# Added products of x in TensorE's order at the norms, the routing and the first gathers of a two-layer decoder trunk

## The reference

```python
def block(x, c, pos, p, cache):
    mod = (jax.nn.silu(c) @ p['w_ada'] + p['b_ada'])[:, None, :]
    shift1, scale1, gate1, shift2, scale2, gate2 = jnp.split(mod, 6, axis=-1)
    h = rmsnorm(x, p['g_norm1']) * (1.0 + scale1) + shift1
    mixed, new_state = token_mixing(h, pos, p, cache)
    x = x + gate1 * mixed
    h = rmsnorm(x, p['g_norm2']) * (1.0 + scale2) + shift2
    x = x + gate2 * hier_moe(h, p['w_router_grp'], p['b_router_grp'], p['w_router_exp'], p['b_router_exp'],
                             p['w_exp_gate'], p['w_exp_up'], p['w_exp_down'])
    return x, new_state
```

## Time and profile before

| | us |
|---|---|
| median of three runs | 2113.04 |
| lowest and highest of them | 2104.05 and 2121.15 |
| the profiled execution's own time | 2108.11 |
| its span from the first to the last instruction | 2106.3 |
| TensorE busy in it | 1872.1 (89%) |
| mean granted clock | 0.931 |

### The profile page before, as it was taken

How to read it: one execution, slowest core, us unless ns; L and a number is a source line. 1 busy time by engine, 2 the same in 40 slices (tenths; PEclk the granted TensorE clock), 3 DMA queues, 4 the chain that set the end, 5 groups by cost and what they waited for, 6 DMA issues and landing times.

```text
span 2106.3 us, 24153 instructions
## 1 busy us (share of the span) xinstructions
PE 1872.1 (89%) x9680; PEld 953.8 (45%) x9680; DVE 555.9 (26%) x1246; ACT 368.5 (17%) x673; POOL 35.3 (2%) x59
## 2 busy tenths in 40 slices
PE   4799667898999999999969994778799999999995
PEld 2477534454444444444436772334444444444442
DVE  0164355533001111011035543554300111101103
ACT  1121134312111010110113102433101101111011
POOL 0000100000000000000000001000000000000000
PEclk9899789889699999999989996989879999999998
DMA  9622389939699999999952208984439999999991
GB/s 399 262 101 71 117 323 342 347 143 365 252 417 375 400 376 382 370 384 392 376 204 80 80 18 295 342 324 185 160 143 416 371 402 375 376 379 369 403 380 82
DMA packets 111863, 609.74 MB, mean 289 GB/s; under 512 B 13219, under 2 KB 15524, under 8 KB 49922
## 3 DMA queue, kind: packets, MB, share of 16 engines
q1 hardware_dynamic: 108690, 595.77, 71.7%
q0 software_dynamic: 3056, 12.35, 1.8%
HBM read 602.26 MB, written 5.81 MB: 289 GB/s over the span
## 4 chain that ended last, share of the span: by engine, by line
PE 75%; SPq 10%; DMA 6%; DVE 4%; issue 3%; ACT 1%; POOL 1%; DVEq 0%; POOLq 0%; ACTq 0%; PEldq 0%
PE PS L1013 31%; PE PS L980 11%; PE PS L591 10%; PE PS L992 7%; SPq L467 5%; SPq L457 4%; PE PS L927 3%; DMA ring<-in_w_ada 3%; PE PS L523 2%; PE PS L549 1%; PE PS L535 1%; DMA ring<-in_w_down 1%; SPq L490 1%; DMA ring<-in_pool_kv 1%; DVE big L1480 1%
## 5 line engine op out<-in xcount | busy, mean ns | idle before, releaser
L1013 PE MATMUL PS<-ring,big 128*64 128x512 f32 x3072 | 680.3, 597 | 6.6 <-ACT big L1152 6.0
L1013 PEld LDWEIGHTS PS<-ring,big 128*64 128x64 f32 x3072 | 214.6, 137 | 427.1 <-issue 418.1
L1152 ACT ACTIVATE big<-PS 128x512 f32<-128x512 f32 (+8 forms) x202 | 145.7, 731 | 1122.1 <-PE PS L1013 394.1
L1480 DVE TENSOR_TENSOR big<-big,PS 128x320 f32<-128x320 f32 (+4 forms) x172 | 88.1, 519 | 741.2 <-PE PS L992 429.0
L980 PE MATMUL PS<-big 128*128 128x256 f32 (+1 forms) x768 | 239.3, 443 | 2.9 <-DVE big L1930 2.2
L591 PE MATMUL PS<-mT,ring 128*128 128x320 f32 x768 | 216.3, 441 | 0.0
L980 PEld LDWEIGHTS PS<-big 128*128 128x128 f32 (+1 forms) x768 | 135.4, 203 | 103.1 <-issue 91.2
L591 PEld LDWEIGHTS PS<-mT,ring 128*128 128x128 f32 x768 | 146.8, 193 | 63.3 <-issue 6.2
L992 PE MATMUL PS<-big 128*128 128x320 f32 x512 | 145.8, 438 | 2.2 <-ACT big L1152 2.2
L992 PEld LDWEIGHTS PS<-big 128*128 128x128 f32 x512 | 94.8, 190 | 62.5 <-issue 22.7
L523 PE MATMUL PS<-cst,big 128*128 128x128 f32 (+4 forms) x472 | 80.5, 296 | 10.5 <-DVEq L389 9.4
(11 more groups left out here) (287 smaller groups left out, 1229.5 us busy)
## 6 DMA issues: line engine op xcount, KB each, us to landing
ring<-in_w_gate SPq DMA_DIRECT2D x128, 1024.0 KB, 9.5
ring<-in_w_up SPq DMA_DIRECT2D x128, 1024.0 KB, 8.7
ring<-in_w_down SPq DMA_DIRECT2D x128, 1024.0 KB, 7.7
ring<-in_pool_kv SPq DMA_DIRECT2D x256, 256.0 KB, 8.7
ring<-in_w_ada SPq DMA_DIRECT2D x48, 1024.0 KB, 14.0
big<-in_windows SPq DMA_DIRECT2D x16, 2432.0 KB, 8.5
ring<-in_w_in SPq DMA_DIRECT2D x24, 1024.0 KB, 7.2
ring<-in_w_out SPq DMA_DIRECT2D x8, 1024.0 KB, 8.6
```

The lines of the kernel that those rows point to most:

```text
L1013: i = mm(PS[SLOTS * x:SLOTS * x + SLOTS, out_bank + half, :], stationary(k, x), w, start=(k == 0), stop=(k == steps - 1))
L1152: return nc.scalar.activation(out, in_, ACT.Copy)
L1480: return V.tensor_tensor(out, a, b, op)
```

## The change

A new function `keep_warm(n)` issues n products of 128 by 128 and 512 columns of x, whose result goes to bank 7 and is read by nobody. They stand in TensorE's list in layer 1 before the tail product (7), before the router product (6), behind the second and the third block of turned rows (2 and 4) and before the first gather (2); in layer 0 before the first gather (4). They wait for nothing. No instruction is taken away, and the other engines' lists stay as they are.

```diff
--- before.py
+++ after.py
@@ -529,6 +529,11 @@
                 half_full(slot, count)
                 pe.wait_ge(ring_full[slot], count * 16)
 
+            def keep_warm(n):
+
+                for _ in range(n):
+                    mm(PS[:, 7, :], xT_[:, 0:128], xT_[:, 0:512], start=True, stop=True)
+
             def add_squares(n, k):
 
                 pe.wait_ge(sem["sq"], KT8 * n + k + 1)
@@ -575,6 +580,8 @@
                     for k in range(KT8):
                         add_squares(2 * l, k)
                 pe.wait_ge(loads, l * LOADS + LOADS_A)
+                if l:
+                    keep_warm(7)
                 for k in range(KT8):
                     pe.wait_ge(sem["h_done"], 2 * KT8 * l + k + 1)
                     i = mm(PS[0:36, 4, 0:T], wtail[:, k, :], mT[:, k, :], start=(k == 0), stop=(k == 7))
@@ -932,6 +939,8 @@
                 add_squares(2 * l + 1, 7)
                 if l == 0:
                     pe.wait_ge(sem["proj_ev"], 32)
+                else:
+                    keep_warm(6)
                 next_mods(3)
                 if l == 0:
                     pe.wait_ge(sem["mod_rows_kept"], 14)
@@ -949,6 +958,8 @@
                     for k in range(KT8):
                         i = tr(PS[0:n, (5, 0, 5)[t] + k // 4, (k % 4) * 128:(k % 4) * 128 + 128], mT[:, k, t0:t0 + n])
                     i.then_inc(sem["rows_turned"], 1)
+                    if l and t:
+                        keep_warm(2 * t)
                 next_mods(2)
                 pe.wait_ge(sem["selected"], l + 1)
 
@@ -967,7 +978,10 @@
                 next_mods(5)
                 if l == 0:
                     mod_turn(23)
+                    keep_warm(4)
                     pe.wait_ge(sem["mods_kept"], 1)
+                else:
+                    keep_warm(2)
                 pe.wait_ge(sem["gates_kept"], l + 1)
                 for part in ((0, 1), (2, 3), (4, 5, 6, 7)):
                     gather(GROUPS * l, part)
```

## The result

| | us |
|---|---|
| before, median of 20 runs | 2113.47 (2101.33 to 2129.41) |
| changed, median of 20 runs | 2086.59 (2080.30 to 2105.66) |
| ratio, with its 95% interval | 0.9869 (0.9849 to 0.9889) |
| profiled execution, before and changed | 2108.11 and 2089.32 |

The change makes the kernel 1.3% faster, and the whole interval lies beyond 1%. The forecast was 2080 in 2070 to 2098.

The account below looks back on a forecast made before the run. TensorE's own work and waits were taken to bound the kernel, with both first gathers at half clock. Gains of 1.9 + 3.2 + 11.9 + 1.4 + 9.6 = 28.0 us took 2108.1 to 2080 us, range 2070 to 2098.

Parts of the forecast that it names:

- The gathers: First gather of each layer: added products keep the clock high, 13.4 us each, gaining 11.9 (layer 1) and 11.5 us (layer 0).
- weights are loaded between the records: Both first gathers: the reason given why 25.3 against 13.4 us is less than a factor of two.
- The second norm and the selection: Layer 1 before the gather: router product 4.50 us instead of 6.68, products 0.6 us too long, ranks' end 3.2 us earlier.
- Layer 0: Four products on the path before its first gather: net gain between 8.4 and 10.8 us, taken as 9.6.
- the list of what the profile would show: Signs expected in the profile after; for layer 0, the added products take 3.5 to 5.6 us.
- The gate products: Behind the first gathers: first 64 gate records at 13.95 us, gaining 1.4 us in layer 1 and 2.1 in layer 0.
- Too short for a fall: Behind layer 1's first gather: 1.97 us of idle TensorE during ScalarE's copy would not lower the clock.
- The tail product: First norm of layer 1: seven hidden products make it 4.50 instead of 6.40 us, 1.9 us gained, ends 0 to 2.1.
- Layer 0 paid: Rival, chance 0.10: the clock falls during layer 0's four products, which cost 2.8 to 5.2 us and bring nothing; 2094 us.
- the clock held through 13.5 us of gather: Rival, chance 0.05, said the opposite: the high clock doesn't hold through a gather of full length; 2107 us.
- the transfers didn't hold up the first group: Rival, chance 0.04, said the opposite: late weight blocks make layer 0's first group wait, taking back its gain; 2090 us.
- The added products never all ran at 1.2 GHz: Rival, chance 0.03, said the opposite: added products run at 1.2 GHz, 1.74 us each, making the kernel slower; 2129.5 us.

## Why the prediction was right

**The gathers: right, and the size too.** The step gave 11.9 and 11.5 us. The profile after has 13.56 and 13.46 us, so 11.7 and 11.5. The Trainium skill's halving (TensorE: Matmul & The Clock Gate, Terms), 12.65 and 12.5, is a little too much here. The prediction's reason, that weights are loaded between the records, is not shown: the gather's weight loads were themselves busy 13.38 us at the low level and 7.77 at the high one. The two experiments that put the levels side by side (inside one gather, and 9 against 512 columns) show the cause.

**The second norm and the selection: right.** The router product took 4.50 us as said. From the last squares to the ranks the stretch shrank from 22.44 to 20.47 us (the step had 20.9), and to the gather from 29.40 to 25.70: 3.7 us gained for a step of 3.2. The products started 0.43 us a record apart, as priced. The selection's copy now ended at 1514.21 and the ranks began at 1514.48. The products were thus 0.3 us too long, not 0.6.

**Layer 0: the mechanism right, the term a little large.** The step had the products start at the high clock and take 3.5 us, or 5.9 where it falls under them (5.6 in the list of what the profile would show). In the profile after the clock was already at 0.50, and they took 5.85. The gather waited for them, and with the gate products the place gave 7.0 us of the step's 9.6: 6.7 of 7.5 ahead of the gate products, 0.4 of 2.1 in them. In the kernel with them alone, where they started high and the gate products kept the clock, it gave 10.9, the upper end of the step; its 9.6 lies between.

**The gate products: wrong.** "Too short for a fall" is the step that failed, 1.4 and 2.1 us in the sum. Of the 2.1 in layer 0 the profile after has 0.4, and in layer 1 the gate products got 0.3 us slower. In the profile after, 1.97 us of idle TensorE was followed by a fall in both layers, 15.65 us each; over all profiles with a gather that ended at the high level and no products behind it, the clock was lost at nine places of ten (15.40 to 16.97 us) and kept at one (13.95). With two added products in the gap it was kept at six of six, at one of them through 1.97 us of idle time all the same.

**The tail product: wrong half the time.** "Far below the 4.1 us that left the clock at 1.00" judged by the length of a gap alone. The same 1.96 us lost the clock in two profiles of four and kept it in two. The 1.9 us are worth about half of that on average; nine products in place of seven made it 4.50 in three of three.

**The sum.** Its parts were 28.0 us and the medians differ by 26.9. The profiled executions alone differ by 18.8: the changed places gave 22.35, and the rest is other stretches that happened to be slower. That 28.0 lies so near 26.9 is in part luck: it holds 3.5 us of gate products and 1.9 of tail product, of which the profile after gave 0.1 and 0.2. The predicted time was nevertheless 6.6 us low, mostly because I added nothing for the 4.9 us by which the profiled execution before lay under the median. My reason, that the two large falls make the scatter and go away, was wrong. The gathers were slow in every profile without dense work ahead, so they added no scatter, and the runs after spread over 25 us, as they did before over 28.

**The rivals.** Layer 0 paid, the clock held through 13.5 us of gather, and the transfers didn't hold up the first group: ScalarE's copy released it in both layers. The added products never all ran at 1.2 GHz. Where the only two did (3.78 us), they still paid.

## What to carry to other kernels

A busy TensorE says nothing of its level: look at the granted clock over each stretch, and for streams whose records are slower than the same form elsewhere. A stream can be unable to bring the clock back and yet keep it, so a few dense products ahead of it can be worth far more than they cost: here 3.78 us of added work took 10.9 us off a gather and 10.7 off the median. What sets the gather apart from the dense products, its 256 columns, its weight loads or something else, no run separates. Put such products first where a wait hides them, and size them by the wait. Two more in the short gap behind the gather kept the clock every time in the profiles; the time doesn't show their gain.

## What the runs showed of the hardware

- A gather busy for 25.20 of 25.20 us (the kernel with 9 columns) stayed at 0.50 all the time. Two dense products in front of it, 3.60 us at 0.50, were enough to have it at 0.93 over its length.
- The same idle gap of 1.96 us behind the same seven products kept the clock in two profiles and lost it in two, while 4.1 us at the second norm had left it at 1.00. And 1.97 to 2.12 us behind a gather lost it at nine places of ten, but 1.97 us behind two dense products kept it at the one place where that was seen. The length of a gap doesn't tell alone; what ran ahead of it and when the clock last rose may count, and no run separates them.
- Behind the two products that follow layer 0's gather, TensorE sat idle 1.31 to 1.97 us with no releaser in the profile (three profiles), which took back most of the 1.7 us that they gave. The cause is open.
